# Hybrid encoder with PEER experts: the tiles of the expert tables move as two half transfers

## The reference

```python
def peer_ffn(h, w_query, sub_keys, expert_u, expert_v):
    ...
        q = (xc @ w_query).reshape(PEER_CHUNK, PEER_HEADS, 2, PEER_HALF)
        sc = jnp.einsum('chpd,hpkd->chpk', q, sub_keys, preferred_element_type=jnp.float32)
        ...
        top_s, pos = lax.top_k(cand_s, PEER_TOPK)
        idx = jnp.take_along_axis(cand_i, pos, axis=-1)
        gate = jax.nn.softmax(top_s, axis=-1)
        u = jnp.take(expert_u, idx, axis=0)
        act = jax.nn.gelu(jnp.einsum('chkd,cd->chk', u, xc, preferred_element_type=jnp.float32),
                          approximate=False)
        vsel = jnp.take(expert_v, idx, axis=0)
        return jnp.einsum('chk,chkd->cd', (gate * act).astype(xc.dtype), vsel)
```

## Time and profile before

| | us |
|---|---|
| median of 3 runs | 4217.31 |
| lowest and highest | 4207.97, 4219.65 |
| profiled execution, its own time | 4213.15 |
| its span on the core | 4211.4 |
| PE busy | 3797.5 (90%) |
| DVE busy | 2332.0 (55%) |
| POOL busy | 708.2 (17%) |
| ACT busy | 429.4 (10%) |

### The profile page before, as it was taken

The page is one execution under the profiler, slowest core; times in us unless marked ns, Lnnn a source line. Parts: engine busy times, 40 slices in busy tenths (PEclk is TensorE's granted clock), DMA queues, the critical chain, the costliest instruction groups (busy, mean ns, idle before and its releaser), DMA issues. The chain is left out here.

```text
span 4211.4 us, 63338 instructions
## 1 busy us (share of the span) xinstructions
PE 3797.5 (90%) x26660; PEld 3415.6 (81%) x26660; DVE 2332.0 (55%) x3749; ACT 429.4 (10%) x1020; POOL 708.2 (17%) x664
## 2 busy tenths in 40 slices
PE   7788789999999999999868878899999999999998
PEld 6576784898999888898856767748989998888987
DVE  3994852794287544424249848527942875443242
ACT  1003220100111000000010132201001110000000
POOL 5530000022011211111055200000210112111110
PEclk9899899999999999999988988899999999999999
DMA  5231014399699999979642300143997999999796
GB/s 169 89 110 29 1 42 149 127 368 400 252 383 380 394 421 421 420 298 421 246 142 89 115 25 1 42 155 131 376 383 259 384 386 402 421 421 413 303 421 245
DMA packets 279468, 1077.39 MB, mean 256 GB/s; under 512 B 46052, under 2 KB 144728, under 8 KB 163992
## 3 DMA queue, kind: packets, MB, share of 16 engines
q1 hardware_dynamic: 223896, 670.72, 42.6%
q0 software_dynamic: 55296, 402.68, 23.4%
HBM read 1071.23 MB, written 2.10 MB: 255 GB/s over the span
## 5 line engine op out<-in xcount | busy, mean ns | idle before, releaser
L1731 PE MATMUL bank<-ex_W,ex_tile 128*128 128x160 f32 x8192 | 1164.6, 302 | 83.9 <-DMA ex_tile<-in_peer_v 83.8
L1731 PEld LDWEIGHTS bank<-ex_W,ex_tile 128*128 128x128 f32 x8192 | 1118.0, 190 | 133.9 <-DMA ex_tile<-in_peer_v 127.0
L1658 PE MATMUL bank<-ycT,ex_tile 128*128 128x160 f32 x8192 | 1155.1, 301 | 47.5 <-DMA ex_tile<-in_peer_uT 47.3
L1658 PEld LDWEIGHTS bank<-ycT,ex_tile 128*128 128x128 f32 x8192 | 1122.6, 191 | 72.3 <-DMA ex_tile<-in_peer_uT 66.7
L1925 DVE SCALAR_TENSOR_TENSOR ex_sums<-ex_row,ex_weight,ex_sums 128x2048 f32<-128x2048 f32 x186 | 437.0, 2349 | 325.8 <-DMA ex_row<-in_peer_v,ex_rows 325.8
L1616 POOL DMA_INDIRECT ex_row<-in_peer_u,ex_rows x192 | 225.3, 1173 | 2084.3 <-DVE ex_rows L1889 1173.3
L1919 DVE CUSTOM_DVE_ANT_0 ex_row<-ex_row,ex_h_wide 128x2048 f32<-128x2048 f32 x192 | 437.4, 2290 | 234.5 <-DMA ex_row<-in_peer_u,ex_rows 232.3
L358 PE MATMUL pj_bank<-pj_hT,pj_piece 128*128 128x256 f32 x2048 | 473.2, 393 | 5.6 <-DMA pj_piece<-in_w_in 3.8
L358 PEld LDWEIGHTS pj_bank<-pj_hT,pj_piece 128*128 128x128 f32 x2048 | 402.9, 198 | 75.6 <-issue 12.0
L1616 POOL DMA_INDIRECT ex_row<-in_peer_v,ex_rows x192 | 188.6, 982 | 1020.9 <-DVE ex_sums L1925 692.2
L813 PE MATMUL bank<-arena,ycT 128*128 128x512 f32 x512 | 222.4, 593 | 2.0 <-PEq L898 2.0
(11 more groups left out here) (376 smaller groups left out, 3149.9 us busy)
## 6 DMA issues: line engine op xcount, KB each, us to landing
ex_tile<-in_peer_uT SPq DMA_DIRECT2D x256, 1024.0 KB, 8.7
ex_tile<-in_peer_v SPq DMA_DIRECT2D x256, 1024.0 KB, 10.2
pj_piece<-in_w_in SPq DMA_DIRECT2D x32, 2048.0 KB, 8.6
arena<-in_w_out SPq DMA_DIRECT2D x16, 2048.0 KB, 8.1
query_w<-in_peer_w_query SPq DMA_DIRECT2D x16, 1024.0 KB, 5.8
ex_row<-in_peer_u,ex_rows POOLq DMA_INDIRECT x192, 14.5
ex_row<-in_peer_v,ex_rows POOLq DMA_INDIRECT x192, 16.9
x<-in_x SPq DMA_DIRECT2D x1, 2048.0 KB, 8.8
```

The source lines that it names most:

```text
L1658: mm = mmul(o, ring[:, j % SLOTS, k * P:k * P + P], hT[k // 4][:, k % 4, 0:DENSE], start=(k == 0), stop=(k == KT - 1))
L1731: mm = mmul(bank[:, at_, lo:lo + DENSE], ring[:, i % SLOTS, m * P:m * P + P], W[:, j, :], start=(j == 0 and m % 3 == 0), stop=(j == TILES ...
```

## The change

Each tile is moved by two DMAs of half the model dimension, 128 partitions by 1024 numbers (4 KB runs where there were 8 KB). Each half of a slot has a `tile_in` semaphore of its own, six for three. PE waits for the first half before block 0 and for the second before block 8, and raises `tile_mm` after each half; SP refills a half slot as soon as that half has been used. ACT waits for two increments per tile. PE's matmuls, the gather, DVE's and ACT's work stay as they are.

```diff
--- before.py
+++ after.py
@@ -1526,7 +1526,7 @@
 
     q_mm, q_out, score_mm, score_out = [sem("ex_" + n) for n in ("q_mm", "q_out", "score_mm", "score_out")]
     rms_wide, rms_mm, h_scaled = sem("ex_rms_wide"), sem("ex_rms_mm"), sem("ex_h_scaled")
-    tile_in, tile_mm, tile_out = [sem(f"ex_tile_in{i}") for i in range(SLOTS)], sem("ex_tile_mm"), sem("ex_tile_out")
+    tile_in, tile_mm, tile_out = [sem(f"ex_tile_in{i}") for i in range(2 * SLOTS)], sem("ex_tile_mm"), sem("ex_tile_out")
     best_ready, exp_ready, picks_ready, picks_mm, picks_out = [sem("ex_" + n) for n in ("best", "exp", "picks", "picks_mm",
                                                                                      "picks_out")]
     hot_ready, gates_mm, gates_put, gates_times, tile_times = [sem("ex_" + n) for n in ("hot", "gates_mm", "gates_put",
@@ -1575,36 +1575,44 @@
         with nc.Block() as block:
             @block.sync
             def _(sp):
-                def u_tile(i, slot, free):
+                half_k = KT // 2
+
+                def u_half(i, slot, h, free):
                     if free is not None:
                         sp.wait_ge(tile_mm, free)
-                    sp.dma_start(ring[:, slot, :], t["peer_uT"][layer, i].rearrange("p k e -> p (k e)"))\
-                        .then_inc(tile_in[slot], 16)
-
-                def v_tile(i, slot, free):
+                    sp.dma_start(ring[:, slot, h * half_k * P:(h + 1) * half_k * P],
+                                 t["peer_uT"][layer, i][:, h * half_k:(h + 1) * half_k, :].rearrange("p k e -> p (k e)"))\
+                        .then_inc(tile_in[2 * slot + h], 16)
+
+                def v_half(i, slot, h, free):
                     sp.wait_ge(tile_mm, free)
-                    sp.dma_start(ring[:, slot, :], t["peer_v"].rearrange("l (i e) d -> l i e d", e=KEYS)[layer, i])\
-                        .then_inc(tile_in[slot], 16)
+                    sp.dma_start(ring[:, slot, h * half_k * P:(h + 1) * half_k * P],
+                                 t["peer_v"].rearrange("l (i e) d -> l i e d", e=KEYS)[layer, i][:, h * D // 2:(h + 1) * D // 2])\
+                        .then_inc(tile_in[2 * slot + h], 16)
 
                 for h in range(WRING, PEER_H):
                     sp.wait_ge(q_mm, h - WRING + 1)
                     query_piece(nc, t, layer, query, sp, h)
                 whole_laps = TILES // SLOTS
-                for i in range(SLOTS):
-                    u_tile(i, i, None)
+                halves = [(e, h) for e in range(SLOTS) for h in range(2)]
+                for e, h in halves:
+                    u_half(e, e, h, None)
                 with sp.Fori(1, whole_laps) as lap:
-                    for e in range(SLOTS):
-                        u_tile(lap * SLOTS + e, e, lap * SLOTS + (e + 1 - SLOTS))
+                    for e, h in halves:
+                        u_half(lap * SLOTS + e, e, h, lap * (2 * SLOTS) + (2 * (e - SLOTS) + h + 1))
                 for i in range(whole_laps * SLOTS, TILES):
-                    u_tile(i, i % SLOTS, i + 1 - SLOTS)
+                    for h in range(2):
+                        u_half(i, i % SLOTS, h, 2 * (i - SLOTS) + h + 1)
                 ahead = SLOTS - TILES % SLOTS
                 for i in range(ahead):
-                    v_tile(i, (TILES + i) % SLOTS, TILES + i + 1 - SLOTS)
+                    for h in range(2):
+                        v_half(i, (TILES + i) % SLOTS, h, 2 * (TILES + i - SLOTS) + h + 1)
                 with sp.Fori(0, (TILES - ahead) // SLOTS) as lap:
-                    for e in range(SLOTS):
-                        v_tile(lap * SLOTS + (ahead + e), e, lap * SLOTS + (TILES + ahead + e + 1 - SLOTS))
+                    for e, h in halves:
+                        v_half(lap * SLOTS + (ahead + e), e, h, lap * (2 * SLOTS) + (2 * (TILES + ahead + e - SLOTS) + h + 1))
                 for i in range(ahead + (TILES - ahead) // SLOTS * SLOTS, TILES):
-                    v_tile(i, (TILES + i) % SLOTS, TILES + i + 1 - SLOTS)
+                    for h in range(2):
+                        v_half(i, (TILES + i) % SLOTS, h, 2 * (TILES + i - SLOTS) + h + 1)
 
             @block.gpsimd
             def _(pool):
@@ -1646,18 +1654,20 @@
                 scores(PEER_H - 1)
 
                 def tile(j):
-                    pe.wait_ge(tile_in[j % SLOTS], 16 * (j // SLOTS + 1))
                     if j >= len(A_BANKS):
                         pe.wait_ge(tile_out, j - len(A_BANKS) + 1)
                     elif j == 2:
                         pe.wait_ge(score_out, TB * PEER_H)
                     o = bank[:, A_BANKS[j % len(A_BANKS)], 0:DENSE]
                     for k in range(KT):
+                        if k % (KT // 2) == 0:
+                            pe.wait_ge(tile_in[2 * (j % SLOTS) + k // (KT // 2)], 16 * (j // SLOTS + 1))
                         if j == 0 and k % 4 == 0:
                             pe.wait_ge(h_scaled, k // 4 + 1)
                         mm = mmul(o, ring[:, j % SLOTS, k * P:k * P + P], hT[k // 4][:, k % 4, 0:DENSE], start=(k == 0),
                                   stop=(k == KT - 1))
-                    mm.then_inc(tile_mm, 1)
+                        if k % (KT // 2) == KT // 2 - 1:
+                            mm.then_inc(tile_mm, 1)
 
                 def gates(g):
                     pe.wait_ge(hot_ready, g + 1)
@@ -1717,7 +1727,6 @@
                 pe.wait_ge(gates_times, GROUPS)
                 for j in range(TILES):
                     i = TILES + j
-                    pe.wait_ge(tile_in[i % SLOTS], 16 * (i // SLOTS + 1))
                     if j >= FIRST:
                         pe.wait_ge(tile_times, j - FIRST + 1)
                     if 0 <= j - WIDEN_2 < 4:
@@ -1726,14 +1735,16 @@
                         fold(1, (j - FOLD_1) // 2)
                     for m in range(KT):
                         at_, lo = OUT_BANKS[m // 3], m % 3 * DENSE
+                        if m % (KT // 2) == 0:
+                            pe.wait_ge(tile_in[2 * (i % SLOTS) + m // (KT // 2)], 16 * (i // SLOTS + 1))
                         if j == 0 and m % 3 == 0 and at_ in A_BANKS:
                             pe.wait_ge(tile_out, TILES)
                         mm = mmul(bank[:, at_, lo:lo + DENSE], ring[:, i % SLOTS, m * P:m * P + P], W[:, j, :],
                                   start=(j == 0 and m % 3 == 0), stop=(j == TILES - 1), skip_group_check=True)
                         if j == TILES - 1 and (m % 3 == 2 or m == KT - 1):
                             mm.then_inc(out_mm, 1)
-                    if j < TILES - 1:
-                        mm.then_inc(tile_mm, 1)
+                        elif m % (KT // 2) == KT // 2 - 1:
+                            mm.then_inc(tile_mm, 1)
 
                 for n in range(4):
                     fold(2, n)
@@ -1766,7 +1777,7 @@
                 scores_out(PEER_H - 1)
 
                 def tile(j):
-                    act.wait_ge(tile_mm, j + 1)
+                    act.wait_ge(tile_mm, 2 * j + 2)
                     a = bank[:, A_BANKS[j % len(A_BANKS)], 0:DENSE]
                     n = min(max(j - FIRST + 1, 0) * GROUP, DENSE)
                     if n:
```

## The result

The changed kernel takes 4370.56 us (median of 4 runs, 4368.02 to 4372.45) beside 4215.69 us for the kernel before on the same chips: a ratio of 1.0378 (95% interval 1.0365 to 1.0392; the two medians by themselves give 1.0367). The forecast was 4430 us, between 4213 and 4490: the sign and the mechanism hold, and the loss is 155 us for the 216 forecast.

A forecast was written before the change was run, and what follows sets the result against it. Full DMA engines, shared by packet turns, were taken to bound the expert stage. Stretch losses of +63, +25, +18, +2 and 0 gave 108 us per layer, 216 in all, on 4213: 4430 us, range 4213 to 4490.

The forecast's parts named there:

- What bounds it: Expert stage: the 16 DMA engines are full where DVE takes rows freely; PE loses 0.6 us per tile there.
- the turns: DMA engines alternate queues packet by packet; 4 KB beside 8 KB leaves SP's queue one third of the bytes.
- Rival 1: Full DMA engines: queues keep equal shares by bytes, leaving only the cost per packet; 4213 to 4233 us, chance 0.17.
- rival 2: Full DMA engines: SP's deeper queue wins share from the gather, so the kernel gets faster; about 4105 us, chance 0.10.
- rival 4: DMA engines: ring's share between one third and half as POOL's queue sometimes empties; about 4320 us, chance 0.10.
- Phase V: Second layer's full stretches 3557 to 3951 and 3991 to 4139: starved tiles add +63 and +25 us.
- DVE's two stops: DVE waits for PE at row 128, some 85 us, and before the fold, some 130 us; adds nothing.
- Phase U: Second layer, 3025 to 3143: 22 rows come early, +18 us; 3439 to 3557, rows tied to tiles: +2 us.
- The failed step: Ring refills in full stretches: the next tile is already queued, so earlier issue gains nothing while engines are full.
- my sum: Stretch losses in the expert stage added up: 108 us per layer, 216 us for both.
- Rival 3: Starved stretches: PE's clock falls to 1.2 GHz, 8.74 us per tile; 4494 us, chance 0.03.
- The packet price: DMA engine time per 4 KB packet: 0.162 us taken, between bounds of 0.158 and 0.186 us.

The follow-up runs named there:

- e2_one_4k: Kernel before, still one transfer, semaphore and wait per tile, but a 64-byte gap in each slot cuts the runs to 4 KB; 4444.43 us, ratio 1.0555.
- e11_early_refill: Changed kernel, but PE waits for both halves before a tile's first product; half slots still freed and refilled early; 4410.85 us, ratio 1.0472.
- e3_rows_4k_too: Changed kernel with each gathered row fetched by two indirect DMAs of 4 KB; 4197.35 us, ratio 0.9966.
- e8_both_4k_whole: Kernel before with whole tiles cut to 4 KB runs by a slot gap, and rows as two 4 KB indirect DMAs; 4251.66 us, ratio 1.0092.
- e4_only_rows_4k: Kernel before with only the gathered rows cut to two 4 KB indirect DMAs, tiles at 8 KB; 4091.9 us, ratio 0.9712.
- e1_by_partition: Two transfers per tile of 64 neighbouring partitions by 8 KB, slots freed and awaited by whole tiles as in the kernel before; 5528.27 us, ratio 1.3133.

## Why the prediction was right, and where it was off

**What bounds it, and the turns: right.** Full engines, shares set by packets in turn, one third for the ring: shown by the periods 3.77 and 3.78 us (forecast 3.82 and 3.82), by the quarters, and by both runs with 4 KB rows. Rival 1 (share by bytes) and rival 2 (share by backlog) are out, the latter also since six halves outstanding got less, not more; so is rival 4, as the full stretch had 4648 packets of the ring to 4535 of the rows.

The shares alone do not say how many packets stand in one turn: one of each or eight of each give the same third. The order of the packets does. In the full stretch of the kernel before (3570 to 3860, 14891 packets on 16 engines, in order of their start) the packet 16 places behind another is of the other queue in 80% of the cases, and the one 32 places behind of the same queue in 70%. That fits engines that change the queue after each packet; with eight to a turn, the packet 16 places behind would mostly be of the same queue. The Trainium skill, "DMA: Bandwidth & Descriptors", section "Queues, rings and completion order", has turns between the queues, which hold here, and some 9 to 17 descriptors in one turn, which by this order do not.

**Phase V: right in size.** Forecast +63 and +25, 88 us per layer; measured 77. To tile 80 it took 450 us for 457 forecast and 396 before; the rest grew by 23, for 25 forecast. DVE's two stops came as worked out.

**Phase U: off.** Forecast +20 per layer, measured +3 and +5. Up to row 16 the rows came no earlier, since DVE was set by its own searches: row 16 was reached 145 us into the phase, 146 before. Only the 13 rows behind it ran at the pace of the engines, in 52 us for 59; the forecast had let all 22 rows of the stretch do so.

**The failed step** is the sentence "An earlier issue finds no idle engine to use", by which the halves' early refill and start were priced at nothing. With no halves at all and the same shares (`e2_one_4k`), V grew by 87 us and U by 20 and 29, some 111 per layer where my sum has 108: the sum was that of a kernel without halves. In U that agreement is partly luck, as row 16 was not reached earlier there either (146 us). The halves then gave back 74 us; 40 are lost without the early start and 26 without the early refill. They give 54 us at equal shares, and nothing where there are no rows. Where it is won can be read: in phase U of the second layer tile 32 comes 148 us after the first tile with halves and 168 with whole ones; in V the difference at the end is 10 us. In that part of U DVE asks for rows between searches, so that the load comes in bursts, and a stall of PE ends sooner if half a tile suffices. That last reason is argued, not shown; the share of 1.00 at only 402 GB/s there should have warned me that this stretch was not full in the sense of V's.

One part of the 74 us may be PE's clock: in its full stretch of V `e2_one_4k` had a granted clock of 0.90, the changed kernel 0.98 to 1.00; over the whole run it was 0.941, and 0.944 in `e11_early_refill`, for 0.963. In the full stretch that cost nothing: the tiles of `e2_one_4k` that start at 3810.59, 3817.83 and 3825.07 take 4.61, 6.29 and 4.61 us and stand 7.24 us apart. Outside it the cost is open. It is not all, since `e3_rows_4k_too` and `e8_both_4k_whole` differ by 54 us at the same clock (0.963 and 0.962). Rival 3 did not occur in the changed kernel. **The packet price** was well placed: 0.162 us taken, 0.162 in the packets' own durations, 0.156 by the periods.

## What to carry to other kernels

When these two DMA queues kept the engines full, the sizes of their contiguous runs set how they shared: to give a transfer priority, keep its runs long and cut the other queue's, as `e4_only_rows_4k` did for 2.9%. Splitting a transfer along the contiguous dimension to start earlier lowered its share against the other busy queue; it was free only with no such queue there (4003.76 and 4001.28 us). Ask who would use the bandwidth that moves: here the gather had slack and spent it standing still.

## What the runs showed of the hardware that I had not expected

- Transfers to 64 neighbouring partitions ran at 252 GB/s in all, at a share of 1.02 (`e1_by_partition`); to every second partition of 128, at 414 GB/s. The row gather, which did not change, slowed down with the ring in the first. The Trainium skill, "DMA: Bandwidth & Descriptors", section "The descriptor swizzle", puts partitions 0 to 63 on one half of the ports and 64 to 127 on the other; the two rates fit that, but no run here shows the ports themselves.
- PE's granted clock fell with quarters and not with halves, and the lower clock hid itself in the stops. In the full stretch of quarters PE at 2.4 GHz worked 1.35 us and stopped 1.81; then the clock fell to 1.2 GHz, and it worked 2.50 us and stopped 0.67. So the short stop is an effect of the lower clock, and no sign of a busier PE. In the mean of that stretch the granted clock was 0.57. With halves PE worked 2.44 us and stopped 1.34, and the clock stayed at 1.00, 2.4 GHz. In that stretch of quarters the lower clock cost nothing, as the portions come each 3.17 us at either clock and the DMA engines set the pace:

```profile
3725.54 1.35 PE L1742 MATMUL bank<-ex_W,ex_tile 128*128 128x160 f32 x8 [1.81 <-DMA ex_tile<-in_peer_v]
3728.70 2.50 PE L1742 MATMUL bank<-ex_W,ex_tile 128*128 128x160 f32 x8 [1.81 <-DMA ex_tile<-in_peer_v]
3731.88 2.50 PE L1742 MATMUL bank<-ex_W,ex_tile 128*128 128x160 f32 x8 [0.68 <-DMA ex_tile<-in_peer_v]
```

```profile
3720.00:3850.00 130.00, 97.30 (x343) 82.39 (x342) 87.64 (x45) 0.74 (x2) 40.90 (x38) 0.57 1.02 413
```
